# Moving columns in alternating 64-byte pieces, and turned operands shifted by 128 bytes

## What is computed

```python
def swiglu(x, wi, wo):
    gate, up = jnp.split(x @ wi, 2, axis=-1)
    return (jax.nn.silu(gate) * up) @ wo

for li in range(2):
    h = h + 0.5 * swiglu(rms_norm(h, ffn1_norm[li]), ffn1_wi[li], ffn1_wo[li])
    h = h + mixer(rms_norm(h, mix_norm[li]))
    h = h + 0.5 * swiglu(rms_norm(h, ffn2_norm[li]), ffn2_wi[li], ffn2_wo[li])
# third layer: the same form, with w_gate, w_up, w_down (1024 x 2816, 2816 x 1024)
```

## Time and profile before

| | |
|---|---|
| median of 3 runs | 1460.09 us |
| the profiled execution's own time | 1459.98 us |
| its span, first to last instruction | 1458.1 us |
| TensorE matmul busy | 1451.5 us (100%), 7822 instructions |
| weight load busy | 1250.3 us (86%) |
| VectorE busy | 1002.2 us (69%) |
| ScalarE busy | 777.7 us (53%) |
| GpSimd busy | 87.1 us (6%) |
| DMA | 266.82 MB, 183 GB/s |

### The profile page before, as it was taken

The page is one execution under the profiler, slowest core; times in us unless marked ns, Lnnn a source line. Parts: engine busy times, 40 slices in busy tenths (PEclk is TensorE's granted clock), DMA queues, the critical chain, the costliest instruction groups (busy, mean ns, idle before and its releaser), DMA issues.

```text
span 1458.1 us, 18627 instructions
## 1 busy us (share of the span) xinstructions
PE 1451.5 (100%) x7822; PEld 1250.3 (86%) x7822; DVE 1002.2 (69%) x1216; ACT 777.7 (53%) x971; POOL 87.1 (6%) x113
## 2 busy tenths in 40 slices
PE   9999999999999999999999999999999999999999
PEld 7888888888888888888888888888888888888887
DVE  6876466777755877459877764787646987687753
ACT  6654355655534555345665544565436876465542
POOL 0000003000000000006100000000000800000000
PEclk9999999999999999999999999999999999999999
DMA  9855563556556555545465556465556543566552
GB/s 328 277 176 185 159 204 116 167 180 201 178 184 200 190 181 195 185 141 172 149 200 188 185 177 206 154 223 182 188 173 217 188 145 118 173 196 201 179 188 72
DMA packets 205620, 266.82 MB, mean 183 GB/s; under 512 B 6944, under 2 KB 148880, under 8 KB 205280
## 3 DMA queue, kind: packets, MB, share of 16 engines
q1 hardware_dynamic: 204320, 261.23, 54.7%
q0 software_dynamic: 1072, 4.35, 0.8%
q10 hardware_dynamic: 144, 0.05, 0.0%
HBM read 264.56 MB, written 1.05 MB: 182 GB/s over the span
## 4 chain that ended last, share of the span: by engine, by line
PE 93%; DVE 3%; ACT 1%; DMA 1%; issue 0%; SPq 0%; DVEq 0%; ACTq 0%
PE ps L631 31%; PE ps L638 17%; PE ps L563 14%; PE ps L565 13%; PE ps L564 13%; PE ps L616 1%; DMA raw<-in_ffn_wi 1%; DVE wlo L1656 1%; PE ps L741 1%; PE ps L836 1%; PE ps L774 1%; DVE d_i L2049 0%; ACT whi L1217 0%; DVE d_m L2045 0%; DVE d_i L2073 0%
## 5 line engine op out<-in xcount | busy, mean ns | idle before, releaser
L1656 DVE TENSOR_TENSOR wlo<-raw,whi 128x2048 fp32r<-128x2048 f32 (+5 forms) x275 | 567.3, 2068 | 259.1 <-ACT whi L1217 258.9
L1217 ACT CAST whi<-raw 128x2048 fp32r<-128x2048 f32 (+5 forms) x275 | 474.0, 1729 | 223.0 <-PE ps L565 218.5
L631 PE MATMUL ps<-xt,whi 128*128 128x512 f32 x2112 | 501.7, 391 | 0.8 <-DVE xt L2249 0.7
L631 PEld LDWEIGHTS ps<-xt,whi 128*128 128x128 f32 x2112 | 389.3, 188 | 78.0 <-DVE xt L2249 1.5
L638 PEld LDWEIGHTS ps<-xt,wlo 128*128 128x128 f32 x2112 | 267.1, 191 | 8.2
L638 PE MATMUL ps<-xt,wlo 128*128 128x256 f32 x2112 | 269.6, 283 | 0.0
L563 PE MATMUL ps<-whi,xt 128*128 128x512 f32 (+4 forms) x304 | 112.7, 371 | 0.0
L565 PE MATMUL ps<-whi,xt 128*128 128x512 f32 (+4 forms) x304 | 109.7, 361 | 0.0
L564 PE MATMUL ps<-wlo,xt 128*128 128x512 f32 (+4 forms) x304 | 109.5, 360 | 0.0
L563 PEld LDWEIGHTS ps<-whi,xt 128*128 128x128 f32 x304 | 57.3, 189 | 9.2 <-issue 1.0
L565 PEld LDWEIGHTS ps<-whi,xt 128*128 128x128 f32 x304 | 57.2, 188 | 8.5
(11 more groups left out here) (422 smaller groups left out, 1884.3 us busy)
## 6 DMA issues: line engine op xcount, KB each, us to landing
raw<-in_ffn_wi SPq DMA_DIRECT2D x85, 1024.0 KB, 5.0
raw<-in_ffn_wo SPq DMA_DIRECT2D x40, 1024.0 KB, 4.9
raw<-in_ffn_w_gate SPq DMA_DIRECT2D x22, 1024.0 KB, 5.1
raw<-in_ffn_w_up SPq DMA_DIRECT2D x22, 1024.0 KB, 5.1
raw<-in_ffn_w_down SPq DMA_DIRECT2D x20, 1024.0 KB, 4.9
raw<-in_w_in SPq DMA_DIRECT2D x14, 1024.0 KB, 5.1
raw<-in_even_w_in SPq DMA_DIRECT2D x6, 1024.0 KB, 5.2
raw<-in_ffn_wo SPq DMA_DIRECT2D x8, 512.0 KB, 3.8
```

The costliest lines, as they stand in the source:

```text
L631: return e.matmul(Pair(job.name).ap[:, b, :], whi[:, v % SPLIT, 256 * j + 128 * b:256 * j + 128 * b + 128], XS[:, j, :, :].rearrange("p h ...
L1217: e.copy(whi[0:n, v % SPLIT, c], raw[0:n, v % RAW, c]).then_inc(s_hi.mark(*[(v, j) for j in js]), 1)
L1656: e.tensor_tensor(wlo[0:n, v % SPLIT, c], raw[0:n, v % RAW, c], whi[0:n, v % SPLIT, c].bitcast(F32), ALU.subtract).then_inc(s_lo.mark(*[(v ...
```

## The change

A new helper `in_step` takes an operand [128, n] with n a multiple of 32 and reads it in another order: 16 columns (64 bytes) from the first half, 16 from the second half, the next 16 from the first, and so on. Operands of another width stay as they are. It is put on the moving operand and on the PSUM output alike in all main products (`steps`, `last_steps`, `by_tiles`, `high`, `low`), so each column still lands at its own place. In `high` the two halves are hi and lo of the k tile. The number and order of the instructions don't change, nor do stationary operands, waits and DMAs.

The buffers of the turned operands get 32 more elements (128 bytes). In `xt` and the FFNs' `ht` (now one buffer with hi and lo behind each other) the data begin after these 32; `yt` (also one buffer now) follows `xt`, and its spare 32 are at its end. So the data of all three begin 128 bytes past a multiple of 256, while `whi` and `wlo` stay at a multiple of 256.

```diff
+def in_step(ap, piece=16):
+
+    n = ap.shape[1]
+    if n % (2 * piece):
+        return ap
+    return ap.rearrange("p (h g i) -> p g h i", h=2, i=piece)
...
-        self.hT = Turned(sb(self.name + "ht_hi", [128, 22, 256], F32R), sb(self.name + "ht_lo", [128, 22, 256], F32R))
+        room = sb(self.name + "ht", [128, 2 * 22 * 256 + 32], F32R)[:, 32:].rearrange("p (h k t) -> p h k t", h=2, k=22)
+        self.hT = Turned(room[:, 0], room[:, 1])
...
-        XS = sb("xt", [128, 8, 2, 256], F32R)
+        XS = sb("xt", [128, 4096 + 32], F32R)[:, 32:].rearrange("p (k h t) -> p k h t", k=8, h=2)
         XT = Turned(XS[:, :, 0, :], XS[:, :, 1, :])
-        YT = Turned(sb("yt_hi", [128, 8, 256], F32R), sb("yt_lo", [128, 8, 256], F32R))
+        yt_room = sb("yt", [128, 4096 + 32], F32R)[:, 0:4096].rearrange("p (h k t) -> p h k t", h=2, k=8)
+        YT = Turned(yt_room[:, 0], yt_room[:, 1])
...
                     h, l = (a[0:n, kt, 128 * tt:128 * tt + 128] for a in (job.act.hi, job.act.lo))
-                    o = pair.ap[:, tt, 0:wd]
+                    o = in_step(pair.ap[:, tt, 0:wd])
+                    hi_w, lo_w = in_step(hi_w), in_step(lo_w)
                     e.matmul(o, h, hi_w, start=i == 0 and j == 0, stop=False)
...
-                    return e.matmul(Pair(job.name).ap[:, b, :], whi[:, v % SPLIT, 256 * j + 128 * b:256 * j + 128 * b + 128],
-                                    XS[:, j, :, :].rearrange("p h t -> p (h t)"), start=j == 0, stop=stop)
+                    return e.matmul(in_step(Pair(job.name).ap[:, b, :]), whi[:, v % SPLIT, 256 * j + 128 * b:256 * j + 128 * b + 128],
+                                    XS[:, j, :, :].rearrange("p h (g i) -> p g h i", i=16), start=j == 0, stop=stop)
...
-                    return e.matmul(Pair(job.name).ap[:, b, 0:256], wlo[:, v % SPLIT, 256 * j + 128 * b:256 * j + 128 * b + 128],
-                                    XS[:, j, 0, :], start=False, stop=stop)
+                    return e.matmul(in_step(Pair(job.name).ap[:, b, 0:256]), wlo[:, v % SPLIT, 256 * j + 128 * b:256 * j + 128 * b + 128],
+                                    in_step(XS[:, j, 0, :]), start=False, stop=stop)
```

More of the change, by code:

```diff
@@ L572, in last_steps @@
                 for tt, c0, n in ((0, 0, wd), (1, 0, wd // 2), (1, wd // 2, wd // 2)):
-                    o = own.ap[:, c0 // (wd // 2), 0:n] if tt else pair.ap[:, 0, :]
+                    o = in_step(own.ap[:, c0 // (wd // 2), 0:n] if tt else pair.ap[:, 0, :])
                     for j in range(nk):
@@ L577, in last_steps @@
                         q.wait_ge(*s_lo[v, j])
-                        hi_w, lo_w = (w[:, v % SPLIT, j * wd + c0:j * wd + c0 + n] for w in (whi, wlo))
+                        hi_w, lo_w = (in_step(w[:, v % SPLIT, j * wd + c0:j * wd + c0 + n]) for w in (whi, wlo))
                         h, l = (a[:, kt, 128 * tt:128 * tt + 128] for a in (job.act.hi, job.act.lo))
@@ L597, in by_tiles @@
                         q.wait_ge(*s_lo[v, j])
-                        hi_w, lo_w = (w[:, v % SPLIT, j * wd:(j + 1) * wd] for w in (whi, wlo))
+                        hi_w, lo_w = (in_step(w[:, v % SPLIT, j * wd:(j + 1) * wd]) for w in (whi, wlo))
                         h, l = (a[:, kt, 128 * tt:128 * tt + 128] for a in (job.act.hi, job.act.lo))
-                        o = pair.ap[:, tt, 0:wd]
+                        o = in_step(pair.ap[:, tt, 0:wd])
                         e.matmul(o, h, hi_w, start=False, stop=False)
```

## The result

The kernel after takes 1517.39 us (1517.17 to 1517.58, 4 runs) where before takes 1460.12 us beside it (1460.01 to 1460.32): slower by the factor 1.0393 (1.0381 to 1.0405). The prediction said 1389 us, 1379 to 1466.

A forecast was written before the change was run, and what follows sets the result against it. The prediction took TensorE's matmul start-to-start distances as the bound: a span of 1458.1 us, less 72.6 gained, plus 2 for waits, gives 1387.5, and with 1.9 around it 1389 us; range over all cases 1379 to 1466.

The forecast's parts named there:

- The bound: On TensorE, the time is the sum of the distances from one matmul's start to the next one's.
- the gain of 72.6 us: Main fp32r products: 4674 of 512 columns save 10.9 ns each, 2280 of 256 columns save 9.5 ns each.
- the 13 ns of the expectations: Part of each fp32r matmul's distance before the change, taken as the same at 512 and 256 columns.
- the 3.4 ns on top of it: What remains on top of the columns in each edited product after the change, taken from inside the fp32 pair.
- the 216.7 and 110.1 ns: Distances forecast after the change for edited products of 512 and 256 columns.
- The 10 ns of the best 360-column place: Upper case for what remains on top of the columns in edited products; the gain would then be 27 us.
- The second step: the pieces: Moving reads and PSUM writes of main products cut into 32 or 16 pieces; the sum gave this no cost.
- the three conditions at the prediction's end: It fails if SBUF isn't interleaved that way, the load doesn't read a column in two clocks, or PSUM minds the jump.
- Half a period apart: Load and moving read in SBUF, starting 128 bytes apart modulo 256 and running at one pace, were not to meet.
- The slower case: Rival, chance 0.21: every piece costs clocks, 32 pieces in a 512-column product and 16 in a 256-column one.
- The case of no change: Rival, chance 0.12: no cause in the reads, so wide products of the main matmuls stay at 227 ns.
- The small terms: Waits in the MLA stretch give back 2 us; fp32 products and evictions unchanged; 144 products of unedited widths under 0.6 us.

The follow-up runs named there:

- half_load: Kernel before with 64 instead of 128 stationary columns loaded in all products of FFNs b1 and c1: 1459.10 us against 1459.84 beside it.
- shift_only: Kernel after with its 128-byte shift kept, but moving operands and PSUM outputs in plain order again: 1480.04 us, factor 1.0138 against before.
- pieces_only: Kernel after with pieces on both sides kept, but the turned operands back at multiples of 256 bytes: 1517.24 us, factor 1.0391 against before.
- load_scan: Kernel before with 32 to 128 stationary columns loaded, differing by FFN, and 64-byte pieces in b1, b2 and the mixers: 1486.84 us.
- walk_scan: Kernel before with another order of the moving read in each FFN (a1: 64-byte pieces, a jump after each, places rising), no shift: 1495.92 us.

## Why the prediction was wrong

- **The bound was right.** TensorE's start-to-start distances are the time: 59.0 us by them, 57.3 by the spans, at a granted clock of 1.00 throughout.
- **The step that failed** is the gain of 72.6 us, 10.9 ns from each wide product and 9.5 from each narrow one: the change gave none of it. It takes a part of the distance for one that every matmul pays alike, whatever its width, the 13 ns of the expectations. The widths don't carry it. The shortest mean distances are 226.7 ns at 512 columns, 160 at 360 (the first k tile, where both operands start at a multiple of 256) and 113.8 at 256 (half_load): 0.443, 0.444 and 0.445 ns a column, and no load and no start in any run brought the mean of the wide products below that. So a wide product has nothing on top of its 0.443 ns a column, and a narrow one 119.6 - 113.8 = 5.8 ns, which came with the load of 128 columns. Only by chance do the two widths of before look like one price. That the 0.443 ns a column are the moving read's own is inferred from these three widths; no run here has no load at all. Sized by width, the wide products had nothing to gain, and the narrow ones at most 6 ns x 2280 = 14 us.
- **The terms of the sum.** No run shows the columns' share that the sum subtracts, and so none shows the 3.4 ns on top of it, nor the 216.7 and 110.1 ns: the shortest means of all runs are 226.7 and 113.8, and after the change they are 240.0 and 120.1. The fp32 pair takes 216.6 and 110.4 ns in the mean at 256 and 128 columns, 0.83 ns a column and 4 ns on top, and says nothing of fp32r. The 10 ns of the best 360-column place aren't shown either: it takes 160 ns, 0.444 a column like the best wide ones. The earlier trace rows shows 0.16 us there and 0.17 later; the other k tiles take 158 to 169 ns, 165 in the mean, so what an address adds there is some 5 ns and not the 10 that two decimals suggest.
- **The second step: the pieces, which the sum puts at nothing.** They cost 57.3 us. Of the three conditions at the prediction's end one held as it stands, PSUM doesn't mind the jump (1480.25 us against 1480.04), and one nearly: the load takes 0.82 ns a column, 1.85 times the 0.443 of the moving side; that this is two clocks no run shows. What it had wrong is that a read near the load's own pace is a free one: the order of the places modulo 256 has a price of its own, 226.7 to 240.1 ns in the down products.
- **Half a period apart was the wrong target.** The address does matter, as the earlier trace rows shows with 0.16 and 0.17 us, but in plain order a difference of 128 bytes costs 4.5 ns on the wide products of gate/up and mixers and 6.1 on those of the down products: shift_only, +20 us. With the change's own pieces it makes no difference whether the turned operands are shifted by 128 bytes (pieces_only 1517.24, after 1517.39).
- **The slower case had the mechanism on one side only.** Measured are 12.4 ns on a wide product of 32 pieces, 0.39 ns a piece, with no gain, and 1517 us. The narrow products, with 16 pieces, paid hardly more than they had already paid for the load (120.1 for 119.65, not 6.2 more): with pieces both widths take 0.469 ns a column (240.0/512, 120.1/256), and with 64 or 32 columns loaded the narrow one stays at 120.0 (load_scan), so the load's part no longer shows. The cost lies in the order of places in SBUF, not in PSUM, and not in pieces as such, since with other places the same 32 pieces are free (226.74 ns, walk_scan, a1).
- **The case of no change** was half right: a wide product got no shorter, whatever was loaded beside it (228.0 with 128 columns, 230.0 with 64, 231.3 with 32), but the change was no neutral reordering of its read.
- **The small terms.** One new wait of 0.6 us came (for `d_v`), the gap ahead of the MLA product shrank instead of growing, and TensorE's waits together shrank by about 1 us, as its products got longer. Unedited widths: fp32 the same; 360 columns, with only their load shifted, 164.1 to 165.5 ns, 48 of them, nothing in the sum. Evictions and the writes of the turned operands: VectorE 1002.2 and 1004.1 us, ScalarE 777.7 both times, as said.
- **The range** ended at 1466 because the slower case entered it only where pieces cost about one clock and the whole gain was there too. The gain and the cost were treated as independent, though both rested on the same unseen behaviour of one read.

## What to carry to other kernels

Take out a candidate for an overhead (here: half of the load) before building a change on it. Comparing widths alone is not enough: over all their starts the main products of before take 119.65 ns at 256 columns, 125.3 at 272, 147.5 at 324, 164.1 at 360 and 227.6 at 512. That is within 1 ns of 12 ns and 0.42 a column, which looks like a fixed price and isn't one. Compare widths at one and the same place modulo 256, and with a small load. Keep the moving operand of an fp32r matmul in plain rising order at least over each 256 bytes: that took 226.7 ns here, and smaller pieces from two halves 236.7 to 250.0. Larger pieces (256 and 512 bytes, 226.7 ns), and 64-byte pieces in PSUM (1480.25 us against 1480.04), were free here. The starts of stationary and moving tiles modulo 256 are worth one scan: here the start of one operand alone gave 0.2%.

## What the runs showed of the hardware

- An fp32r matmul of 512 columns took 226.7 ns at best in the mean, at a granted clock of 1.00, over all loads and starts tried, 0.443 ns a column; one of 360 took 160 in the first k tile; one of 256 113.8 with a load of 64 columns and 119.6 with 128.
- A smaller load can make a wide matmul slower: 228.0 with 128 stationary columns, 230.0 with 64, 231.3 with 32 (gate/up products). Why stays open.
- A weight load takes 109 ns for 32 columns, 134 for 64, 161 for 96 and 188 for 128: 0.82 ns a column. 99% of them start within 0.01 us of a matmul's start (before).
- Where the load starts against the moving read, modulo 256, moves a wide product between 226.7 ns (0) and 234.3 (96).
- Reading every second column halves the pace (451.4 ns), and every fourth hardly more (461.6).
- 64-byte pieces that alternate between two halves of the moving operand take 240 ns for 512 columns where 226.7 to 228 stood; in PSUM they cost nothing (1480.25 us against 1480.04).
